# Second block on VectorE: q's first rotations after the scan's bank reads, the first k block after the last states

## What is computed

```python
xn = rmsnorm(h, norm1_gain[i])
proj = xn @ w_in[i]
q, k, v, u, gates = jnp.split(proj, splits, axis=-1)
q = rope(rmsnorm(q, q_norm_gain[i]), cos, sin)     # 8 heads x 2 x 64 columns
k = rope(rmsnorm(k, k_norm_gain[i]), cos, sin)
...
s = s5_layer(u, ...)      # linear recurrence over the tokens, 32 groups x 64 states
```

## Time and profile before

| what | us |
|---|---|
| median of three runs | 2069.97 (2069.93 to 2071.17) |
| the profiled execution, as timed | 2067.69 |
| its span in the profile | 2065.9 |
| TensorE busy in the span | 2027.7 (98%) |
| VectorE, ScalarE, GpSimd busy | 1323.9, 942.2, 945.9 |

### The profile page before, as it was taken

One profiled execution on the slowest core, in us unless ns is written; L12 is line 12 of the kernel. 1 busy time (PEld: TensorE's weight loads), 2 busy tenths in 40 slices (PEclk: granted clock), 3 DMA queues, 4 the chain that ended last, 5 costly groups with the idle time before them and its releaser, 6 DMA issues.

```text
span 2065.9 us, 27849 instructions
## 1 busy us (share of the span) xinstructions
PE 2027.7 (98%) x10072; PEld 1629.6 (79%) x10072; DVE 1323.9 (64%) x1979; ACT 942.2 (46%) x1385; POOL 945.9 (46%) x368
## 2 busy tenths in 40 slices
PE   8999999999999999999999998999999999999999
PEld 7875788888888775888888887878776888888887
DVE  5866257787757654268877749975688625464555
ACT  6345464443453446544344353355576444333332
POOL 5433246544645323756566656234322354443442
PEclk9999999999999999999999999999999999999999
DMA  5432213332224331123233333332211323233222
GB/s 189 155 113 74 69 62 102 104 120 99 91 85 155 123 90 62 62 85 118 90 103 111 104 116 103 92 106 94 77 47 62 116 88 101 83 101 102 90 94 82
DMA packets 111858, 202.29 MB, mean 98 GB/s; under 512 B 6544, under 2 KB 51856, under 8 KB 111504
## 3 DMA queue, kind: packets, MB, share of 16 engines
q1 hardware_dynamic: 104800, 189.12, 28.0%
q10 hardware_dynamic: 6960, 11.88, 2.0%
HBM read 189.44 MB, written 8.12 MB: 96 GB/s over the span
## 4 chain that ended last, share of the span: by engine, by line
PE 80%; DVE 10%; issue 4%; ACT 3%; POOL 2%; ACTq 0%; DMA 0%; DVEq 0%; SPq 0%; POOLq 0%
PE bank L796 46%; PE bank L1043 13%; PE bank L1023 7%; PE bank L910 6%; PE bank L1054 2%; PE bank L921 2%; DVE att L2826 1%; POOL w_lo L602 1%; PE bank L868 1%; PE bank L939 1%; DVE att L2809 1%; PE bank L979 1%; DVE w L2686 1%; PE bank L967 1%; PE bank L850 1%
## 5 line engine op out<-in xcount | busy, mean ns | idle before, releaser
L602 POOL TENSOR_TENSOR w_lo<-raw,w_hi 128x2048 fp32r<-128x2048 f32 (+1 forms) x123 | 542.6, 4411 | 827.0 <-ACT w_hi L1544 812.4
L796 PE MATMUL bank<-act_hi,w_hi 128*128 128x512 f32 x1072 | 427.6, 399 | 1.6 <-DVE hid L2894 1.3
L796 PE MATMUL bank<-act_hi,w_lo 128*128 128x512 f32 x1072 | 418.2, 390 | 0.0
L796 PE MATMUL bank<-act_lo,w_hi 128*128 128x512 f32 x1072 | 417.9, 390 | 0.0
L1544 ACT ACTIVATE w_hi<-raw 128x2048 fp32r<-128x2048 f32 (+1 forms) x112 | 203.3, 1815 | 281.0 <-PE bank L796 195.9
L796 PEld LDWEIGHTS bank<-act_hi,w_hi 128*128 128x128 f32 x1072 | 201.5, 188 | 54.6 <-issue 12.4
L796 PEld LDWEIGHTS bank<-act_hi,w_lo 128*128 128x128 f32 x1072 | 201.3, 188 | 43.3
L796 PEld LDWEIGHTS bank<-act_lo,w_hi 128*128 128x128 f32 x1072 | 201.6, 188 | 40.6 <-issue 1.0
L570 POOL TENSOR_TENSOR w_lo<-w_sum,w_hi 128x1024 fp32r<-128x1024 f32 x56 | 133.6, 2406 | 206.0 <-ACT w_hi L1853 192.5
L2563 DVE TENSOR_TENSOR f<-f,bank 128x512 f32<-128x512 f32 x196 | 133.4, 686 | 111.1 <-PE bank L1043 111.1
L1043 PE MATMUL bank<-w_hi,q_hi 128*128 128x512 f32 x392 | 152.7, 390 | 0.5 <-DVE w_lo L2570 0.4
(11 more groups left out here) (427 smaller groups left out, 4131.4 us busy)
## 6 DMA issues: line engine op xcount, KB each, us to landing
raw<-in_w_up SPq DMA_DIRECT2D x32, 1024.0 KB, 5.6
raw<-in_w_down SPq DMA_DIRECT2D x32, 1024.0 KB, 4.9
raw<-in_w_in SPq DMA_DIRECT2D x26, 1024.0 KB, 5.2
raw<-in_w_up SPq DMA_DIRECT2D x44, 512.0 KB, 4.5
raw<-in_w_in SPq DMA_DIRECT2D x28, 768.0 KB, 4.6
raw<-in_w_out SPq DMA_DIRECT2D x12, 1024.0 KB, 5.0
raw<-in_w_down SPq DMA_DIRECT2D x22, 512.0 KB, 4.1
raw<-in_w_attn_proj SPq DMA_DIRECT2D x4, 1024.0 KB, 4.9
```

Source lines behind the costliest of these rows:

```text
L602: pool.tensor_tensor(m.w_lo[slot][:, 0:n], m.raw[slot][:, 0:n], m.w_hi[slot][:, 0:n].bitcast(F32), ALU.subtract).then_inc(s["split_ready"], 1)
L796: mm = pe.matmul(o, ll if i == 2 else lh, rl if i == 1 else rh, start=first and n == 0, stop=last and n == len(steps) - 1)
```

## The change

Only VectorE's order changes. The out-reading of the first q columns goes from step 9 to step 11. The first rotations of q go from steps 8, 9, 12 and 13 to 11, 12, 12 and 13, so rotation 0 stands behind stage 2 of the first block's states, and rotation 1 behind the bank reads and sums of the second block's. `column_root` and the first k block go from step 22 to step 23, behind `skip` and the last stage of the last block's states. The other engines keep their order: ScalarE and TensorE use `K_AT`, `PARTNER_AT` and `COLUMNS_AT` as before.

```diff
-COLUMNS_OUT_AT = (9, 19)
+COLUMNS_OUT_AT = (11, 19)
 K_AT = (22, 24, 26, 28, 30, 36, 38, 42)
+K_OUT_AT = (23,) + K_AT[1:]
 PARTNER_AT = (6, 7, 10, 11, 14, 15, 18, 19, 21, 23, 24, 26, 29, 34, 36, 40)
-ROTATE_AT = (8, 9, 12, 13, 16, 17, 20, 21)
+ROTATE_AT = (11, 12, 12, 13, 16, 17, 20, 21)
...
         for j in jobs_at(p, ROTATE_AT):
             rotate(j)
-        if p == COLUMN_ROOT_AT + 2:
+        if p == COLUMN_ROOT_AT + 3:
             column_root()
-        for j in jobs_at(p, K_AT):
+        for j in jobs_at(p, K_OUT_AT):
             k_block(j)
```

## The result

The kernel after takes 2079.14 us (median of six runs, 2077.62 to 2081.13), the kernel before beside it 2070.57 (six runs, 2068.66 to 2071.96): a ratio of 1.0046, 95% interval 1.0036 to 1.0057. The change makes the kernel slower by 8.6 us where I had forecast 4.85. The direction was right; the time lies 0.1 us above the range.

The account below looks back on a forecast made before the run. TensorE, busy 98%, was taken to bound the kernel, losing time in waits on VectorE's queue, itself held by GpSimd. 7.8 + 1.35 - 4.3 = +4.85 us on 2069.97 gave 2074.8, range 2069.5 to 2079.0.

Parts of the forecast that it names:

- Part 1: q's later rotations: the unit's `w_lo` comes late, accumulation 16 starts 2.7 us later; with clock loss +4.05 us at accumulation 17.
- the lock: VectorE and GpSimd exclude each other for whole instructions on SBUF's port pair; first eight scans take 8.1 us.
- sharing: Alternative for the port pair: VectorE and GpSimd share bandwidth, so the eight scans take some 4 us.
- Rival 1: First eight scans slip past GpSimd at 2.63 us; +1.05 us, 2071.0, not slower; chance 0.20.
- The first failed step: the clock: TensorE's lower clock behind the unit's wait and behind hook 24's wait: 1.35 us lost each, bounds 0 to 3.1.
- The second failed step: the hold at step 20: Block 3's stage 0 follows TensorE, held less by `w_lo` than now; rotation 7 ends 3.45 us later, at 1336.2.
- Part 2: First k block: wait at line 1188 goes, -4.3 us; hook 24 passes 7.8 us later for bank 7, plus 1.35 clock.
- Dearer: Slow fetch issue (+1.2), longer scans (+0.8), lower clock twice as long (+1.7): +8.6 us, 2078.5; chance 0.17.
- The plain reading: Both TensorE waits, lines 1181 and 1188, go and nothing is late behind: -11.8 us, 2058.2; chance 0.08.
- Only the k half hidden: The root comes earlier than read, so q's +4.05 us meets -4.3 at line 1188: 2069.7; chance 0.07.

Follow-up runs that it names:

- q half alone: Kernel before with only q's columns and rotations moved; `column_root` and first k block stay at step 22: 2074.77 us, ratio 1.0020.
- the short `w_lo`: Kernel after with GpSimd's `w_lo` of step 20 made for 64 of 2048 columns, the rest left out: 2075.06 us, ratio 1.0029.
- both terms taken out together: Kernel after with step 20's `w_lo` cut to 64 columns and idle TensorE products (13, 15, 10) in its waits: 2072.33 us, ratio 1.0010.
- k half alone: Kernel before with only `column_root` and the first k block moved to step 23, all of q as before: 2070.52 us, ratio 1.0005.

## Why the prediction was right in sign and short in size

**Part 1, step by step.** Scans of 8.1 us under six table products: 7.90. Columns out at 1277.05: 1277.65 - 0.96 = 1276.7. Hook 12's wait of 4.1: 3.9. The unit's copy at 1292.05: 1292.76 - 0.96 = 1291.8, behind four issues that followed rotation 1. `w_lo` ready at 1298.55: 1299.25 - 0.96 = 1298.3. Accumulation 16 at 1298.6 behind 5.6: 1298.35 behind 5.06. `skip` of block 0 at 1300.5: 1301.17 - 0.96 = 1300.2. The times of this walk held within 0.4 us. At hook 14 I expected a wait of about 1; there was none, as TensorE lost 1.7 us of clock behind hook 12 and came later itself.

The rule on the port pair ("SBUF — State Buffer" of the Trainium skill, "SBUF: two separate sides") priced the scans right: 7.90 is near the 8.1 that I had worked out by the lock, and not the 4 of sharing. Rival 1, with its short holds, is out: rotation 1 ended at 1290.19 - 0.96 = 1289.2, not before 1287.5.

**The first failed step: the clock.** I took 1.35 us behind the unit's wait and again behind hook 24's, from the two waits of before. Measured were 2.7 and 3.2. At hook 24 that is 3.2 - 1.35 = 1.8 us of excess outright. The other one reached VectorE: TensorE was 5.2 us late at hook 19 instead of 4.05, VectorE stood 1.56 us for its matmuls of line 1204, and the second q columns came 4.5 us late instead of the 3.45 of the forecast. The q half alone shows what the clock did there: it lost only 1.3 us behind the unit's wait, as forecast, and its second q columns (line 2713, at 1317.38, in an execution 2.0 us early) came 3.5 us late. So 1.0 us of rotation 7's delay is clock as well. My range had 3.1 as the far bound of this term, and I held the likeliest value to be that of before, though in before the clock had fallen 2 us into the wait and here it fell just before the end.

**The second failed step: the hold at step 20.** "Block 3's stage 0 is set by TensorE, and as the unit's `w_lo` holds it less than now, rotation 7 ends at 1332.77 + 3.45 = 1336.2." It ended at 1341.07 - 0.96 = 1340.1, 3.9 us later, and stage 0 was not set by TensorE: its matmuls of line 1169 were through at 1326.26, and stage 0 began at 1329.97, straight behind the held sum. VectorE came to stage 2 of block 2 about 4.5 us late; then line 2698 was held for 4.25 us where before a sum was held for 1.24: 4.5 + 3.0 = 7.5, against a measured delay of 7.4 and my 3.45. I had looked at `w_lo`'s length and not at which instruction of VectorE it would meet. With the short `w_lo` the hold, and with it some 3.5 us, went, so the cause is shown, not only read.

**Part 2** was right in mechanism: bank 7 free through `column_root`, ScalarE's root and the refining, 1349.62 - 1345.96 = 3.66 us (0.80 + 2.03 + 0.79 = 3.62 forecast), and the wait ahead of 1188 gone. With rotation 7 at 1340.1 hook 24 is passed 11.84 us later than before instead of 7.8, behind 5.3 us of waiting instead of 3.7.

**The sum.** 11.84 + 3.2 - 4.3 = 10.7, where the profile shows 10.6 and the forecast 4.85: +4.0 from the later bank at hook 24 (3.0 of it the hold, 1.0 the clock behind the unit's wait) and +1.8 from the clock behind hook 24. With both terms taken out together the rest came out as summed, 3.5 us, so no other term of size was wrong. The runs' medians differ by 8.6, 2 us less than the two profiled executions; before's own runs spread over 3.3 us, its profiled one lies below all six timed beside after, and how much clock is lost isn't the same in each execution (1.5 or 2.9 us behind the same 6.0 us wait of hook 14, in before and in the k half alone). How the 2 us are shared out stays open.

**The rivals.** "Dearer" (2078.5) came nearest to the time, but not by its means: its slow fetch and its longer scans didn't come, its clock did, and the hold at step 20, which no rival had, made up the rest. That its +8.6 is the measured figure is luck. "The plain reading" fell by the waits at 796 and 1214. "Only the k half hidden" fell as well: hook 24 was late.

## What to carry to other kernels

Before you move work of VectorE, follow every consumer of its semaphores on the other queues, and walk on to where each of GpSimd's long instructions will stand: the question is which instruction of VectorE it meets, since one that reads PSUM passes and one with both inputs in SBUF stands for its whole length. When a step is moved off a critical stretch, move only the instruction that has no waiter: the k half as made changed nothing that can be told; with `column_root` left in place and the request for the bank one hook later it won 5.8. Price an idle gap of TensorE by a range for the clock behind it, here 0 to 3.2 us a gap, not by the value of one gap.

## What the runs showed of the hardware

- The granted clock fell about 2 us into before's waits of 6.0 and 3.0 us, but some 4 to 5 us into after's three. What a gap of 3 to 6.8 us cost behind itself went from 0 to 3.2 us and hardly followed the gap's length: 1.3 behind 3.0, 0 behind 3.3 (line 1188 in the q half alone), 1.7 behind 3.9, 2.7 behind 5.06, 3.2 behind 5.3, 3.1 behind 6.8, and behind the same 6.0 once 1.5 (before) and once 2.9 (the k half alone).
- 0.24 us decided over about 3 us: `w_lo` starting 0.05 us behind the last sum left it at 0.69 us, starting 0.19 us ahead made it 4.94. It was 4.95 in five other kernels. Another such instruction of the kernel before took 5.05 us.
- Moving GpSimd's six table products away from the scans sped these up (4.90 to 2.63 us) and made the kernel 3.0 us slower (1 to 5 by the interval).
- Products whose result nobody reads, put into the waits, brought the granted clock from 0.91 to 1.00 in two stretches, but only from 0.94 to 0.96 in the one between, and 2.5 us of the time by the medians.
